# Laying out the on-chip tiles anew so that most begin at the same place modulo 1024 bytes

## The reference, cut to what matters

```python
def swiglu(h, w1, w3, w2):
    return (jax.nn.silu(h @ w1) * (h @ w3)) @ w2
...
for l in range(DEPTH):
    x = x + 0.5 * swiglu(rms_norm(x, ffn1_norm[l]), ffn1_w1[l], ffn1_w3[l], ffn1_w2[l])
    h = rms_norm(x, mix_norm[l])
    z = h @ w_in[l]
    ...
    x = x + mixed @ w_out[l]
    x = x + 0.5 * swiglu(rms_norm(x, ffn2_norm[l]), ffn2_w1[l], ffn2_w3[l], ffn2_w2[l])
```

## The kernel before

| tile | bytes a partition | start before | modulo 1024 |
|---|---|---|---|
| raw, whi, wlo | 24576 each | 16512, 41088, 65664 | 128 |
| x | 8200 | 90240 | 128 |
| hT_all | 16384 | 98464 | 160 |
| X | 40960 | 114848 | 160 |
| G | 24576 | 155808 | 160 |
| Y | 24576 | 180384 | 160 |
| KEEP | 13824 | 204960 | 160 |
| consts | 4548 | 218784 | 672 |
| st, par, ident_r | 1024, 3072, 512 | 223360, 224384, 227456 | 128 |
| mask_r | 1024 | 227968 | 640 |

## Time and profile before

### The profile page before, as it was taken

How to read it: one execution, slowest core, us unless ns; L and a number is a source line. 1 busy time by engine, 2 the same in 40 slices (tenths; PEclk the granted TensorE clock), 3 DMA queues, 4 the chain that set the end, 5 groups by cost and what they waited for, 6 DMA issues and landing times. The chain is left out here.

```text
span 1721.3 us, 24478 instructions
## 1 busy us (share of the span) xinstructions
PE 1670.2 (97%) x9754; PEld 1421.3 (83%) x9754; DVE 1160.4 (67%) x1343; ACT 817.5 (47%) x1109; POOL 229.6 (13%) x204
## 2 busy tenths in 40 slices
PE   7999999999999999999999999999999998999898
PEld 6888788889988887888878887978887977787785
DVE  5766757665766666676666765777666487657875
ACT  5443546643454444444455653454344443644453
POOL 0000240010000000000050010000000087004920
PEclk9999999999999999999999999999999888998999
DMA  7657454433546554656555332555655452255411
GB/s 234 221 173 235 147 181 148 145 118 111 184 134 209 193 175 145 222 182 210 186 172 183 107 130 74 183 171 187 207 181 176 138 172 73 86 166 157 157 56 61
DMA packets 207888, 274.94 MB, mean 160 GB/s; under 512 B 19030, under 2 KB 168376, under 8 KB 207288
## 3 DMA queue, kind: packets, MB, share of 16 engines
q1 hardware_dynamic: 206376, 272.67, 49.5%
q10 hardware_dynamic: 1424, 1.05, 0.3%
HBM read 271.61 MB, written 1.08 MB: 158 GB/s over the span
## 5 line engine op out<-in xcount | busy, mean ns | idle before, releaser
L436 DVE TENSOR_TENSOR wlo<-raw,whi 128x2048 fp32r<-128x2048 f32 (+1 forms) x258 | 582.0, 2258 | 250.0 <-ACT whi L425 249.8
L425 ACT ACTIVATE whi<-raw 128x2048 fp32r<-128x2048 f32 (+1 forms) x258 | 483.9, 1879 | 244.1 <-PE banks L553 54.0
L505 PE MATMUL banks<-hT_all,whi 128*128 128x512 f32 x1408 | 493.8, 393 | 2.1 <-DVE hT_all L355 0.9
L506 PE MATMUL banks<-hT_all,wlo 128*128 128x256 f32 x1408 | 397.3, 282 | 0.0
L505 PEld LDWEIGHTS banks<-hT_all,whi 128*128 128x128 f32 x1408 | 265.0, 188 | 61.1 <-issue 1.8
L506 PEld LDWEIGHTS banks<-hT_all,wlo 128*128 128x128 f32 x1408 | 266.7, 189 | 1.6
L553 PE MATMUL banks<-whi,Y 128*128 128x512 f32 x704 | 229.1, 396 | 1.8 <-DVE Y L682 1.8
L553 PEld LDWEIGHTS banks<-whi,Y 128*128 128x128 f32 x704 | 132.3, 188 | 34.8 <-issue 3.5
L998 PE MATMUL banks<-hT_all,whi 128*128 128x256 f32 x896 | 160.7, 282 | 0.1
L309 POOL TENSOR_TENSOR st<-st 128x1 f32<-128x1 f32 x18 | 18.6, 1038 | 960.9 <-ACT X L302 960.9
L998 PEld LDWEIGHTS banks<-hT_all,whi 128*128 128x128 f32 x896 | 136.7, 188 | 3.8 <-issue 3.6
(11 more groups left out here) (374 smaller groups left out, 2460.3 us busy)
## 6 DMA issues: line engine op xcount, KB each, us to landing
raw<-in_ffn_w SPq DMA_DIRECT2D x132, 1024.0 KB, 5.5
raw<-in_w_in SPq DMA_DIRECT2D x80, 1024.0 KB, 5.5
raw<-in_w_out SPq DMA_DIRECT2D x16, 1024.0 KB, 4.9
raw<-in_w_br_na SPq DMA_DIRECT2D x4, 1024.0 KB, 5.1
raw<-in_w_br_mla SPq DMA_DIRECT2D x4, 1024.0 KB, 5.0
raw<-in_w_br_gla SPq DMA_DIRECT2D x4, 1024.0 KB, 5.1
raw<-in_cmp_k_w SPq DMA_DIRECT2D x4, 1024.0 KB, 7.8
raw<-in_cmp_v_w SPq DMA_DIRECT2D x4, 1024.0 KB, 5.5
```

Source lines behind the costliest of these rows:

```text
L425: act.activation(m["whi"][:, slot, 0:w], m["raw"][:, slot, 0:w], ACT.Copy).then_inc(s.hi_ready, 1)
L436: dve.tensor_tensor(m["wlo"][:, slot, 0:w], m["raw"][:, slot, 0:w], m["whi"][:, slot, 0:w].bitcast(F32), ALU.subtract).then_inc(s.lo_ready, 1)
L505: pe.matmul(B[bank + mt][:, :], hi, self.m["hT_all"][:, kk, :], start=n == 0, stop=False)
L506: mm = pe.matmul(B[bank + mt][:, 0:T], lo, self.m["hT_all"][:, kk, 0:T], start=False, stop=n == KK - 1)
```

## The change

Two allocations move. `Y` goes to the place behind `wlo`, ahead of `X` and `G`; `hT_all` comes behind `G`; and `x`, the only tile here with a size that is no multiple of 32 bytes and the one that put the tiles behind it off by 32 bytes, goes to the end. No instruction is added, removed, reshaped or moved in its engine's order. No tile changes its size.

```diff
         wlo = sb("wlo", [P, RING, UNIT], F32R)
-        x = sb("x", [P, NT, D + 1])
+        Y = sb("Y", [P, 12, 2, T], F32R)
+        X = sb("X", [P, 10240])
+        G = sb("G", [P, 24 * T])
         hT_all = sb("hT_all", [P, KK, 2 * T], F32R)
         hT_hi, hT_lo = hT_all[:, :, 0:T], hT_all[:, :, T:2 * T]
-        X = sb("X", [P, 10240])
-        G = sb("G", [P, 24 * T])
-        Y = sb("Y", [P, 12, 2, T], F32R)
         KEEP = sb("KEEP", [P, 3456])
         consts = sb("consts", [P, CONSTS.shape[1]])
         st = sb("st", [P, 256])
         par = sb("par", [P, 768])
         ident_r = sb("ident_r", [P, P], F32R)
         mask_r = sb("mask_r", [P, T], F32R)
+        x = sb("x", [P, NT, D + 1])
```

## The result

The changed kernel takes 1724.39 us (median of 20 runs, 1721.45 to 1727.60), the one before, measured beside it, 1719.69 (20 runs, 1714.99 to 1723.78). The ratio is 1.0028, with a 95% interval of 1.0020 to 1.0036: slower by 4.7 us. That is inside the 0.3% that the prediction called no change, but clear of zero, and the forecast was zero. So the question is where 4.7 us come from in a program that has the same instructions.

A forecast was written before the change was run, and what follows sets the result against it. TensorE's matmul pace was taken to bound the kernel. Four terms of 0 summed to 0, so the forecast stayed at the median of 1719 us, with a range of 1708 to 1727 us.

The forecast's parts named there:

- the 0.3% that the prediction called no change: Whole kernel: about what a measurement can tell from no change, 5.2 us of the median; no change had chance 0.64.
- What bounds the kernel: TensorE, busy 97% of the span with 9754 matmuls: only their pace or new holes can move the time.
- three comparisons say it does not depend on where operands begin: TensorE's matmul streams: about 8% of unexplained pace was held independent of operand starts, so the term was 0 us.
- A shift of 512 bytes changes nothing: Up unit pairs: stationary weights of the second eight begin 512 bytes further, yet pairs stay at 0.347 us.
- second comparison: 256- and 512-column matmuls: the pace is alike whichever tile moves, 396 ns for 512 columns against `Y` or `hT_all`.
- third: L2199 loads 32 stationary columns instead of 128, yet takes 0.458 ns a column against 0.455 in the down unit.
- Neighbours, VectorE, ScalarE, `x` and the small tiles at 0: Tiles' new places and neighbours, the other engines and shifted small tiles: 0 us, with +-1 us for the load of `x`.
- slower pairs at +5 to +9 us: Rival at L505 and L506: reads meet, pairs stay at 350 to 353 ns; 1726 us, chance 0.08.
- faster 512-column matmuls at -6 for L553 and L987 and a third more for smaller lines: Rival of a faster pace at distance 0: some 4 ns a matmul, -6 to -9 us in all, 1711 us; chance 0.15.
- the prediction's own sign of being wrong: Timeline paces of pairs, down units, matmul groups and VectorE's subtraction: any moved, even by 3 ns, means distance matters.
- the opening mode: First three pairs of an up unit, 0.350 us each against 0.347 settled; staying there would cost +5 to +9 us.
- The rule of the Trainium skill: Matmul pace: 325 ns a pair where the trace has 347; removing the excess would save 31 us in up units.

The follow-up runs named there:

- pad32: The changed kernel with 32 unused bytes ahead of `Y`, so `Y` and `hT_all` are again 32 bytes off the weights: 1718.69 us, 1.000 of before.

## Why the prediction was wrong

- *What bounds the kernel* was right: TensorE's pace, 0.53 ns a matmul for 0.3%. The whole result is changes of pace.
- *The failed step* is "three comparisons say it does not depend on where operands begin", and in it the first: "A shift of 512 bytes changes nothing". That is true, and says nothing about 32 bytes (pairs went from 347.2 to 352.6 ns when those went): 512 is twice 256, and modulo 256 the two halves of a unit lie at the same distance. I had compared a distance with itself. The term that was put at 0 on this ground measured +7.6 us in the pairs, +7.9 in the 256-column matmuls and -11.0 where weights move.
- The *second comparison* (which tile moves) compared moving operands 32 bytes after the stationary one with moving operands 32 bytes ahead of it. Before, 256 columns took 117.1 with `hT_all` moving and 116.9 with weights moving; at distance 0 they take 119.8 and 114.6. The agreement at 32 bytes was a coincidence of that distance.
- The *third* (32 stationary columns instead of 128) speaks of the size of the load and not of places: the same line went from 116.9 to 114.6 with the distance. It was no clean test of the size either. The blocks of 32 columns begin 128 bytes apart, so before the change they lay by turns 32 and 160 bytes off the weights modulo 256.
- *Neighbours, VectorE, ScalarE, `x` and the small tiles at 0* were right: pad32, which leaves all of these as changed but for 32 bytes, is at 1.000 of before, and VectorE's 681 and 686 ns are those of before within 1.
- *The rivals* were both half right, and their prices close: slower pairs at +5 to +9 us, measured +7.6; faster 512-column matmuls at -6 for L553 and L987 and a third more for smaller lines, measured -7.3 and -3.2. I had put them down as alternatives. They came together, with 256-column matmuls 2.7 to 3.1 ns slower besides (+7.9 us), a term that the prediction had not named. A sum of two bounds of opposite sign is no proof of zero.
- *Luck.* The time, 1724.39 us, lies inside the range of 1708 to 1727 because 15.4 and 11.0 us nearly cancel, not because the paces stood. By the prediction's own sign of being wrong, any pace moved by 3 ns, it was wrong. The price of the slower pairs was right for another reason than the one given: the pairs did not stay in the opening mode. That mode is 352, 353 and 352 ns (the prediction read 350 from rounded starts); the settled pairs of the changed kernel take 349, 350 and 361 in turn. The range was also 1 us short for its own bound, +9 us on 1719.
- *The clock* was no part of it: the two profiled executions were granted 0.983 after and 0.982 before, and their spans still differ by 4.2 us.
- *The rule of the Trainium skill* ("TensorE: Matmul & The Clock Gate", section "Back-to-back issue gap") is N / 2.4 + 2.5 ns for isolated matmuls, as the prediction says; these stand back to back. At the best distance seen, 512 columns take 227 ns, not 216. The traces do not reach its figure at any distance tried, though part of the excess, 6 ns of 17, does go by the layout.

## What to carry to other kernels

In a kernel whose TensorE streams 4-byte operands without a hole, the starts of tiles are a parameter. What counts here is the distance, modulo 256 bytes as far as tried, between the moving tile and the stationary one. It is worth 2 to 3% of a matmul's pace, and the best distance differs between forms; the stream ahead and, in pairs, the second weight tile have a part in it too. "All aligned alike" is not the optimum; put each pair of tiles at the distance that suits the form which uses it most, and measure it by starts in the timeline, because gains and losses hide in each other's sum (here 15.4 us against 11.0). A comparison inside one trace clears a cause only if it varies that cause: state what the compared distance is modulo small powers of two before leaning on it.

## What was not expected of the hardware

- The paces above: at equal clock (2.4 GHz granted in these stretches) and with nothing waiting, the same 512 columns take 227.0 or 233.3 ns and the same 768-column pair 347.2 or 353.2. The Trainium skill, "SBUF — State Buffer", section "Who interferes with whom", gives TensorE two read ports of its own, one for the moving operand and one for the weight load, independent of each other. The runs here show that where the two operands begin against each other changes the pace; the measurement decides. Whether it is the two reads that meet is not shown: a matmul with a quarter of the weight load changed its pace as well (116.9 to 114.6 ns), and the attempt to tell which of the two weight tiles holds up which matmul had no clear answer. The mechanism stays open.
- A stream has a memory. After the change the matmuls of a down unit take 0.233 us each on average for the first 11, scattered between 224 and 241 ns, and a steady 0.227 from then on; with the same distance of `Y`, but behind up units of another pace, only the first three are slow (229.1 against 227.4 ns on average). At 64 bytes one line has two paces, 113 and 118 ns for 256 columns, in neighbouring stretches with the same tiles; that the matmuls ahead pick between these two is not shown.
